# First attention: where the probabilities of heads 10 to 15 are divided by their rows' sums

## The reference, cut to what matters

```python
# global, per head and block of 128 queries
s = jnp.einsum('bqkgd,bskd->bkgqs', qi, k) * scale
p = jax.nn.softmax(s, axis=-1)
o = jnp.einsum('bkgqs,bskd->bqkgd', p, v)
# window: keys within 128 of the query, and a sink in the denominator
m = jnp.maximum(jnp.max(s, axis=-1, keepdims=True), sink_l)
e = jnp.exp(s - m)
den = jnp.sum(e, axis=-1, keepdims=True) + jnp.exp(sink_l - m)
p = e / den
o = jnp.einsum('bnkgqc,bnckd->bqkgd', p, vb)
...
mixed = concatenate([rms_norm(out_a, ...), rms_norm(out_b, ...)]) @ w_out
```

## Time and profile before

| what | value |
|---|---|
| median of 3 runs | 1130.67 us (1129.24 to 1130.89) |
| profiled execution | 1130.22 us |
| its span | 1128.4 us |
| PE, DVE, ACT, POOL busy | 97%, 74%, 54%, 11% of the span |
| first attention | ticks end near 190 us of the span |

### The profile page before, as it was taken

The page is one execution under the profiler, slowest core; times in us unless marked ns, Lnnn a source line. Parts: engine busy times, 40 slices in busy tenths (PEclk is TensorE's granted clock), DMA queues, the critical chain, the costliest instruction groups (busy, mean ns, idle before and its releaser), DMA issues.

```text
span 1128.4 us, 18209 instructions
## 1 busy us (share of the span) xinstructions
PE 1096.7 (97%) x6856; PEld 974.9 (86%) x6856; DVE 831.4 (74%) x1424; ACT 613.4 (54%) x1109; POOL 121.5 (11%) x143
## 2 busy tenths in 40 slices
PE   8999989998999999999999999999999999999997
PEld 6788777998999999888898887787899999988886
DVE  6898886788988888733378688664799988875333
ACT  6787884576555555422254468544555555562331
POOL 1476743000000000000000004200000000000000
PEclk9999999999999999999999999999999999999999
DMA  7423312321333333433323321032233333343312
GB/s 281 121 63 92 93 39 100 107 76 54 129 97 97 113 113 112 116 109 112 110 68 113 93 57 38 19 94 60 90 111 105 98 100 113 113 131 100 105 57 75
DMA packets 34150, 109.30 MB, mean 97 GB/s; under 512 B 4368, under 2 KB 7056, under 8 KB 33936
## 3 DMA queue, kind: packets, MB, share of 16 engines
q1 hardware_dynamic: 33312, 107.22, 30.9%
q10 hardware_dynamic: 752, 0.92, 0.3%
HBM read 100.78 MB, written 2.10 MB: 91 GB/s over the span
## 4 chain that ended last, share of the span: by engine, by line
PE 84%; DVE 7%; ACT 5%; issue 2%; POOL 1%; DMA 1%; ACTq 0%; SPq 0%; DVEq 0%; POOLq 0%
PE bank L544 12%; PE bank L545 12%; PE bank L546 12%; PE bank L2097 10%; PE bank L2099 10%; PE bank L2098 10%; PE bank L1061 2%; PE bank L1051 2%; PE bank L1006 1%; PE bank L1134 1%; PE bank L1008 1%; PE bank L1007 1%; PE bank L1136 1%; PE bank L1135 1%; DVE wl L465 1%
## 5 line engine op out<-in xcount | busy, mean ns | idle before, releaser
L465 DVE TENSOR_TENSOR wl<-raw,wh 128x1024 fp32r<-128x1024 f32 x109 | 135.2, 1242 | 146.4 <-ACT wh L457 146.1
L457 ACT ACTIVATE wh<-raw 128x1024 fp32r<-128x1024 f32 x109 | 114.6, 1054 | 182.4 <-PE bank L546 169.8
L2097 PE MATMUL bank<-h,wh 128*128 128x256 f32 x576 | 163.5, 284 | 3.5 <-ACT acc L2438 1.8
L2099 PE MATMUL bank<-h,wl 128*128 128x256 f32 x576 | 163.0, 283 | 0.0
L2098 PE MATMUL bank<-h,wh 128*128 128x256 f32 x576 | 163.0, 283 | 0.0
L2097 PE MATMUL bank<-hh,wh 128*128 128x256 f32 x432 | 122.5, 283 | 2.1 <-ACT acc L2450 2.1
L2098 PE MATMUL bank<-hl,wh 128*128 128x256 f32 x432 | 122.2, 283 | 0.0
L2099 PE MATMUL bank<-hh,wl 128*128 128x256 f32 x432 | 122.2, 283 | 0.0
L544 PE MATMUL bank<-hh,wh 128*128 128x512 f32 x296 | 119.4, 403 | 2.4 <-DVE wl L465 1.4
L544 PE MATMUL bank<-gh,wh 128*128 128x512 f32 x308 | 119.8, 389 | 0.0
L545 PE MATMUL bank<-gl,wh 128*128 128x512 f32 x308 | 119.8, 389 | 0.0
(11 more groups left out here) (293 smaller groups left out, 2656.3 us busy)
## 6 DMA issues: line engine op xcount, KB each, us to landing
raw<-weights SPq DMA_DIRECT2D x181, 512.0 KB, 3.7
xres<-x_t SPq DMA_DIRECT2D x8, 512.0 KB, 6.2
sw<-ta SPq DMA_DIRECT2D x36, 64.0 KB, 2.0
out_t<-final SPq DMA_DIRECT2D x6, 256.0 KB, 2.1
q<-sw SPq DMA_DIRECT2D x10, 128.0 KB, 2.3
q<-ta SPq DMA_DIRECT2D x10, 128.0 KB, 2.3
rope<-angles SPq DMA_DIRECT2D x1, 1024.0 KB, 10.0
sw<-ta ACTq DMA_DIRECT2D x4, 64.0 KB, 3.2
```

Source lines behind the costliest of these rows:

```text
L457: act.activation(wh[:, j, :, :], raw[:, j, :, :], ACT.Copy).then_inc(high_split, 1)
L465: v.tensor_tensor(wl[:, j, :, :], raw[:, j, :, :], wh[:, j, :, :].bitcast(F32), ALU.subtract)\
L2097: pe.matmul(o, wh_half[:, h, k, :], high[:, k, :], start=first and k == 0, stop=False, skip_group_check=True)
L2099: ins = pe.matmul(o, wl_half[:, h, k, :], high[:, k, :], start=False, stop=k == HK - 1, skip_group_check=True)
```

## The change

From head 10 on (`LATE`) the four multiplications of a head are issued by VectorE, right behind the reciprocal, and no longer by GpSimd. VectorE first waits for its own reciprocal (`inverted`), and at head 10 also until GpSimd has scaled the 40 blocks of the heads before, so that `normed` counts in order. The operation, its tiles and sizes are the same. In all 24 instructions move: 12 of 128x256 and 12 of 128x384. The multiplications of heads 0 to 9 stay where they are.

```diff
+LATE = 10
...
+        def scale_row(eng, n):
+
+            s, j = n // 4, n % 4
+            lo, hi = key_range(HEADS1[s][0], j)
+            p = pr1[:, s % PR1, j, lo * P:hi * P]
+            eng.tensor_scalar(p, p, rden[:, n % 8:n % 8 + 1], 1.0, ALU.mult, ALU.mult).then_inc(at1.normed, 1)
+
         def vec_tick(v, t):
...
                 v.reciprocal(rden[:, c], rsum[:, c]).then_inc(at1.inverted, 1)
+                if s >= LATE:
+                    v.wait_ge(at1.inverted, s + 1)
+                    if s == LATE:
+                        v.wait_ge(at1.normed, 4 * s)
+                    for n in range(4 * s, 4 * s + 4):
+                        scale_row(v, n)
...
         def gpsimd_tick(g, t):
             if t % 4 == 1 and 4 < t <= STEPS + 1:
                 for n in range(t - 5, t - 1):
-                    s, j = n // 4, n % 4
-                    lo, hi = key_range(HEADS1[s][0], j)
-                    p = pr1[:, s % PR1, j, lo * P:hi * P]
-                    g.wait_ge(at1.inverted, s + 1)
-                    g.tensor_scalar(p, p, rden[:, n % 8:n % 8 + 1], 1.0, ALU.mult, ALU.mult).then_inc(at1.normed, 1)
+                    if n < 4 * LATE:
+                        g.wait_ge(at1.inverted, n // 4 + 1)
+                        scale_row(g, n)
```

## The result

The changed kernel takes 1136.91 us in the median of 6 runs (1135.34 to 1138.07), the kernel before 1129.95 us in 6 runs beside them (1128.85 to 1130.93). The ratio is 1.006, 95% interval 1.005 to 1.007: slower, by 6.9 us. The forecast was slower by 2.8 us, with a range up to 1136.6. The sign was right, the size was not, and the measured median lies above the range.

The account below looks back on a forecast made before the run. PE, 97% busy, was taken as the bound, held up in the first attention mostly by VectorE. Terms 1.5 + 0.1 + 1.2 + 0.1 - 0.4 + 0.3 = +2.8 us; forecast median 1133.3 us, range 1130.2 to 1136.6.

Parts of the forecast that it names:

- What bounds: First attention, 130 to 190 us: PE is held up mostly by VectorE, which has no room; GpSimd isn't the bound.
- signs named: Scalings near 0.3-0.4 us, VectorE full 138-156 us, output 1.5 us later, wait before 168.43 over 2 us, `mix` below 1.49.
- signs of being wrong: PE's VectorE waits no longer, scalings swallowed by gaps or 0.7 us or more, clock 1.00 near 150 or falling near 170.
- N: VectorE's added time for one head, four scalings plus the wait on its reciprocal: 1.2 us.
- (a): Heads 10 and 11, from 138.65 us to PE's first output piece: two N less a 0.94 us gap, +1.5 us.
- (f): GpSimd's RoPE steps, near 138 to 141 us, and squares, about 150 to 155, newly clash with VectorE: +0.3 us (0 to 2).
- (b): Heads 12 and 13, 150 to 165 us: PE full, VectorE has 2.3 us free against 2.4 of work, +0.1 us.
- (c): Head 14, 165 to 171 us: VectorE sets the tick's length, so N goes on the path whole, +1.2 us.
- (d): Head 15 at 171.01 us: PE full, VectorE has 1.7 us free for 1.2, +0.1 us.
- (e): VectorE's `mix` at 175.78 us gets shorter as most of GpSimd's squares run earlier: -0.4 us (0 to -0.75).
- second rival: Clash: each scaling or `mix_l` that meets a GpSimd step waits for it; +4.5 us, 1135.2; chance 0.12.
- third rival: PE's longer wait near the end brings a second clock fall costing 1.7 us; +4.5 us, 1135.2; chance 0.08.

Follow-up runs that it names:

- no_meetings: The change, with GpSimd's last RoPE sine and sum held until head 10 is scaled and squares of tiles 3 to 6 until head 15 is: 1135.06 us.
- head_14: The kernel before with only head 14's scalings moved to VectorE: 1132.10 us against 1129.61.
- head_14_filled: The kernel before with only head 14 scaled on VectorE, plus ten matmuls in PE's wait (output not the reference's): 1131.13 us against 1130.06.
- filled: The whole change plus ten matmuls in PE's wait at tick 64 (output not the reference's): 1136.30 us against 1130.06.
- squares_early: The kernel before with GpSimd's squares of tiles 3, 4 and 5 moved to earlier queue gaps: 1129.18 us against 1130.06; again 1130.30 against 1129.48.
- rope_held: The change, with GpSimd's sine and sum of the last RoPE tile held until head 10 is scaled: 1136.57 us against 1129.48.
- squares_held: The change, with GpSimd's squares of tiles 3 to 6 held until head 15 is scaled: 1136.61 us against 1129.61.
- spread: The change, with each head's four scalings split into two pairs at the ends of two later ticks: 1139.55 us against 1130.06.

## Why the prediction was wrong, point by point

**What bounds.** Right: VectorE is what PE waits for in this stretch, and GpSimd's place on the chain of before was worth nothing. ScalarE's stall and PE's 1.0 us wait for head 11 went, and no time with them. Of the signs named, three came: VectorE is full (5.93 or 5.94 us of each 6 from 138 to 156), the wait before 168.43 grew to over 2 us, `mix` of tile 6 is below 1.49. Two of the signs of being wrong came as well: single scalings of up to 1.30 us (a meeting) and a second fall of the clock.

**N.** 1.3 us, against 1.2: from the reciprocal at 147.26 to the maxima at 148.66 are 1.40 us, 0.10 of which was there before. Single scalings are 350 and 415 ns (335 and 400 foreseen). The fast slope was right: 65 ns for 128 columns against 67.

**(a) heads 10 and 11.** Foreseen +1.5 for two N less the gap; in no_meetings PE's first output piece comes 1.5 us later than before. Right, as far as this term goes: in the changed kernel it is 2.7, by the meeting that belongs to (f).

**(b) heads 12 and 13.** Foreseen +0.1. Head 13 costs nothing, head 12 costs its 1.3 us whole. This step failed: I compared 2.3 us of gaps summed over 15 us with 2.4 us of work, but the gaps lie behind 156 us, and head 12's work comes at 154 us, where VectorE had none. Of the gaps 1.2 us lie between the reciprocals of heads 12 and 13, and most of that was the work of the fall, which makes PE late and VectorE wait for it: in head_14, whose clock does not fall, 0.3 us are left there. So the fall hid 1.0 us of the price. A sum over a long stretch says nothing about the place.

**(c) head 14.** Foreseen +1.2, 1.3 measured (head_14_filled, no_meetings). Right.

**(d) head 15.** Foreseen +0.1. No run has head 15 by itself; in filled, where PE's clock is at 1.00 there, the path from head 15's reciprocal to PE's sum is 0.2 us shorter than before, with a `mix` that is 0.4 us shorter (1.10 us). So the scaling costs about 0.2, if the `mix` counts in full. Right, as far as that shows it.

**(e) the end.** Foreseen -0.4 (0 to -0.75); `mix` went from 1.49 to 0.91, -0.6. Right. That the end gains this much no run shows: head_14 and squares_early, with shorter `mix` too, don't have it in their times.

**(f) meetings.** Foreseen +0.3 (0 to 2), the most mis-sized term of the sum: it measured 2.5 in the marks of the trace. Head 10's meeting with RoPE costs 1.2 us (rope_held), the squares' with `mix_l` 1.3 us up to head 14 (squares_held): together 2.5. I had the mechanism, its places and the steps that move there, and its price for one: the excess of 0.75 us of one `mix`. What I got wrong is how many there would be. The trace has four: the sink's addition 0.2 us, the scalings of head 10 1.0, `mix_l` of tile 1 0.9, of tile 2 0.3, 2.4 together, and each falls where VectorE had no gap. The price of one is not bounded by 0.75 us either: `mix_l` of tile 1 has 0.9, and a single scaling beside a GpSimd step 1.0. It was the second rival, with 0.12. The size is that of single traces: filled has some 0.5 us less for the squares, and by the medians both kinds together are worth 1.3 to 1.6 us (no_meetings), each kind by itself nothing that can be told (rope_held, squares_held).

**The clock.** Left out of the sum, the third rival with 0.08; a term put at nothing. It came: PE's wait near the end is 2.66 us and the clock falls behind it, as it does behind head_14's wait of 2.49 us and not when that wait is filled. In the kernel before, the runs beside the experiments show what a fall is worth: 20 runs with a mean clock of 0.999 average 1129.0 us, 32 with 0.997 average 1130.0, 6 with 0.994 or 0.995 average 1131.2. That is 1.0 to 1.2 us for each of these steps down in the mean clock, less than the 1.7 of the third rival. The mean clock of these runs is 0.9974, of the changed kernel's six 0.9937. The forecast took the two rivals as alternatives, each alone at +4.5; they came together. That the meetings, by longer waits, helped to bring the falls is likely and not shown: no_meetings has a second fall too, behind a wait of 2.49 us.

Summed from the runs, by the marks of the profiled executions up to head 15's reciprocal: 1.3 for heads 10 and 11 without meetings, 1.3 for head 12, 1.3 for head 14, 2.5 for the meetings: 6.4, against 6.5 in the changed kernel (5.55, and 0.97 for the fall of before read out). From there to PE's sum it loses 1.0 more, where filled, without a fall there, is 0.2 faster than before. These 1.2 us, and 0.2 for the `mix` that is shorter by so much here than in filled, are the second fall, 1.4 us. In the prediction's terms three steps failed: (b), put at 0.1, is 1.3 in place of it; (f), put at 0.3, is 2.5 in this trace; and the second fall, put at nothing, is about 1.4. Against them stands the fall of before, 1.0, which the change no longer has in that place.

What is left open is how much of the difference between the medians, 6.9 us, belongs to the meetings and how much to the falls. Only one execution of each kernel has a trace (squares_early has two), and filled and squares_early show that meetings and falls both differ from one execution of the same instructions to the next.

## What to carry to other kernels

Moving work from an idle engine to a busy one is priced at the place: ask at the very instruction behind it how long that engine has until someone waits, not what its gaps sum to. When GpSimd and VectorE work out of SBUF, an engine that is relieved starts its next steps earlier, so list what runs beside what afterwards, and take up to a whole step of the other engine for each instruction that meets one. Where a change lengthens PE's waits, the price of a fall of its clock belongs into the sum. And a fall in the trace of before makes gaps on the other engines that are gone when it does not come.

## What the runs showed of the hardware

A VectorE scaling of 128x256 or 128x384 in place, with a per-row operand, takes 350 or 415 ns; a pair, one of each, takes 0.67 us alone and 2.6 us beside two GpSimd steps of 1.04 and 1.27 us, which keep their length there (spread). Which engine takes longer is not fixed: where a `mix_l` and a GpSimd step begin within 0.05 us of each other, the `mix_l` took 1.63 us and the step 1.04 in the changed kernel, 0.75 and 1.61 in filled. An addition of four columns (128x4) with two SBUF inputs takes 0.39 us beside GpSimd's RoPE step, 0.86 beside a step of the squares (squares_early), and 0.15 without. And the mean granted clock of one and the same program, the kernel before, is 0.999 in some executions and 0.994 in others, with 2 us between their times (1129.0 and 1131.0 on average): the falls of PE's clock are not the same from one execution to the next.
